# Local attention in a two-block kernel: the second round of transposes starts in another PSUM bank, and one operand split moves one step later

## The chip, the cores and the metric

The kernel runs on one core of a Trainium2 chip. The metric is the time of one execution on the device in microseconds (us). Lower is better. TensorE is called PE in the profile, VectorE DVE, ScalarE ACT, GpSimd POOL and SyncE SP.

## The reference, cut to what matters

The whole program computes two transformer blocks on 512 tokens of width 1024. The first has two kinds of attention and a mixture of experts. The second has a short convolution beside a local (windowed) attention, and then a large product-key feed-forward network. The change lies in the mixer of the second block:

```python
WINDOW = 128
BLOCK = 128
N_HEADS = 8
N_KV_HEADS = 2

def short_conv(b_gate, c_gate, h, conv_w):
    u = c_gate * h
    ...
    y = conv_w[0] * up[:, 0:s]
    for j in range(1, CONV_K):
        y = y + conv_w[j] * up[:, j:j + s]
    return b_gate * y

def window_attention(q, k, v, rel_bias, sinks):
    nb = s // BLOCK
    ...
    kw = with_prev(kb)
    vw = with_prev(vb)
    scores = jnp.einsum('bnqkgd,bnjkd->bnkgqj', qb, kw).astype(jnp.float32) * (HEAD_DIM ** -0.5)
    ...
    m = jnp.maximum(scores.max(axis=-1), sink)
    p = jnp.exp(scores - m[..., None])
    denom = p.sum(axis=-1) + jnp.exp(sink - m)
    o = jnp.einsum('bnkgqj,bnjkd->bnkgqd', p, vw.astype(jnp.float32)) / denom[..., None]

y_conv = short_conv(b_gate, c_gate, hc, conv_w[l])
y_attn = window_attention(q, k, v, rel_bias, sinks[l])
mixed = concatenate([group_rms_norm(y_conv, ...), group_rms_norm(y_attn, ...)])
x = x + g1[:, None] * (mixed @ w_out[l])
```

There are four query blocks of 128 tokens, numbered n = 0 to 3. Each looks at its own 128 keys and, except block 0, at the 128 before them.

## The kernel before

The order of the work is written out by hand: for each stage there is one function per engine (`mix_pe`, `mix_ac`, `mix_dv`), each engine runs its own list in order, and semaphores join them. `F.pe`, `F.ac` and `F.dv` are the counters of the mixer stage. `F.ac["pt", n, kc, 0]` names the point at which ACT has done its copy for block n, key half kc, group 0. `wait_ge` on it holds the engine until that point.

The heart of the mixer is a loop over i = 0 to 11 that all three engines run in step. In step i PE computes the projection chunk 6 + i (`project`, L2232, 24 matmuls of 128x512). Each chunk needs its weights split in two rounded parts by ACT (L2189) and DVE (L2203); `ahead(9 + i)` makes one such pair per step. Between the projections stand the pieces of attention, by the tables `SCORE`, `TURNED`, `VALUES`, `MEANS` and `SCALES`:

- `score(n)`: PE computes the scores of block n (L2275, eight heads in PSUM banks 0 to 3, two heads in each bank). DVE adds the bias and writes them to S8 (L2528), then takes the maximum. ACT takes the exponentials (`exponentials`, L2414).
- `turned(n)`: PE transposes the probabilities (L2291, four 128x128 transposes to a group). For a block with two key halves there are four groups: kc = 0 and kc = 1, each with g = 0 and g = 1. Groups with g = 0 go to bank 6 and are copied out by ACT (L2424), groups with g = 1 go to bank 7 and are copied out by DVE (L2544).
- `values(n)`: PE multiplies with the values into bank 6 (L2301), ACT copies and squares the result (L2436, L2437).
- `means(r)` (L2310, L2313, then L2556, L2557 on DVE, a square root L2441 on ACT and a reciprocal L2559 on DVE), `scales(r)` (L2068 on PE) and `normed(r)` (L2563, L2567 on DVE) are the group norms. ACT's `normed` and DVE's `split` (L2446, L2574) round the result for the output product.
- In the steps 2, 5, 8 and 11 DVE also makes a convolution channel block, `yc` (L2599, L2602, L2606).
- `conv_split(0)` rounds the first half of the normalised convolution for the output product: a copy on ACT (L2455) and a subtraction on DVE (L2580).

After the loop PE runs `begin(0)` and `begin(1)`, the first output products (L2232 again, 6 matmuls each), which read what `conv_split(0)` made, then `scales(2)`, `values(3)`, `begin(2)`, `means(3)`, `begin(3)` and `scales(3)`. The rest of the output product is L2383.

Blocks 1, 2 and 3 are turned in the steps i = 6, 9 and 11. The text calls these place 1, place 2 and place 3.

Of the kernel before, what the change touches and what calls it, by code (L numbers as in the profile page):

```python
# [12 lines left out]
ACT = mybir.ActivationFunctionType  # L13
# [165 lines left out]
def build(nc, A, ctx):  # L179
    with nc.sbuf_tensor("arena", [128, ARENA], F32) as AR:  # L180
        pass
    PS = ctx.enter_context(nc.psum_tensor("psum", [128, 8, 512], F32))
# [41 lines left out]
    IDENT = CST[:, C_ID:C_ID + 128]  # L224
# [1795 lines left out]
    FN, F = Stage(counter, "final", "pe ac dv"), Stage(counter, "mix", "pe ac dv")  # L2020
# [21 lines left out]
    S8 = at3(o, 8, 256)  # L2042
# [171 lines left out]
    def width(n):  # L2214

        return (0, 256) if n else (1, 128)

    def mix_pe(pe):
        final_pe(pe)
        before = [None] * 8  # L2220

        def claim(b):
            if before[b] is not None:
                pe.wait_ge(*before[b])
# [35 lines left out]
        def score(n):  # L2260
            kc0, nk = width(n)
            if n:
                pe.wait_ge(*F.dv["score", n - 1])
                if n == 2:
                    pe.wait_ge(*F.dv["normed", 0])
                if n == 3:
                    pe.wait_ge(*F.dv["normed", 1])
            else:
                pe.wait_ge(*F.dv["q mean"])
                pe.wait_ge(*F.dv["v"])  # L2270
                pe.wait_ge(*F.dv["keys"])
                pe.wait_ge(*F.dv["first", 7])
            for h in range(8):
                j, g = h % 4, h // 4
                pe.matmul(PS[:, h // 2, 256 * (h % 2) + 128 * kc0:256 * (h % 2) + 256],  # L2275
                          Q2[64 * g:64 * g + 64, j, 128 * n:128 * n + 128],
                          K2[64 * g:64 * g + 64, 128 * n + 128 - nk:128 * n + 128], True, True).then_inc(*F.pe("score", n, h))
                if h in (3, 7):
                    pe.wait_ge(*F.pe["score", n, h])

        def turned(n):
            kc0, _ = width(n)
            for kc in range(kc0, 2):
                for g in range(2):
                    if kc == kc0:
                        pe.wait_ge(*F.ac["exp", n])
                        claim(6 + g)
                    else:
                        pe.wait_ge(*(F.dv if g else F.ac)["pt", n, 0, g])
                    for j in range(4):  # L2290
                        ins = pe.transpose(PS[:, 6 + g, 128 * j:128 * j + 128], S8[:, 4 * g + j, 128 * kc:128 * kc + 128], IDENT)  # L2291
                    ins.then_inc(*F.pe("pt", n, kc, g))
            before[6], before[7] = F.ac["pt", n, 1, 0], F.dv["pt", n, 1, 1]

        def values(n):
            kc0, _ = width(n)
# [94 lines left out]
    def mix_ac(ac):  # L2391
        ahead = splits_ac(ac)
        final_ac(ac, ahead)
        ahead(4)
        ac.wait_ge(*F.pe["chunk", 0])
        ac.activation(K2, PS[:, 0, :], ACT.Copy).then_inc(*F.ac("k"))
        ac.activation(KSQ, PS[:, 0, :], ACT.Square).then_inc(*F.ac("k square"))
        ac.wait_ge(*F.pe["chunk", 1])
        ac.activation(VST, PS[:, 1, :], ACT.Copy).then_inc(*F.ac("v"))
        for j in range(4):  # L2400
            ahead(5 + j)
            if j == 2:
                ac.wait_ge(*F.dv["k mean"])
                ac.activation(W1[:, 32:40], W1[:, 32:40], ACT.Sqrt, scale=64.0).then_inc(*F.ac("k root"))
            ac.wait_ge(*F.pe["chunk", 2 + j])
            ac.activation(Q2[:, j, :], PS[:, 4 + j, :], ACT.Copy).then_inc(*F.ac("q", j))
            ac.activation(SQ4[j], PS[:, 4 + j, :], ACT.Square).then_inc(*F.ac("q square", j))

        def exponentials(n):
            kc0, _ = width(n)  # L2410
            ac.wait_ge(*F.dv["max", n])
            ac.activation(ST[:, 16:24], ST[:, 8:16], ACT.Exp)
            for h in range(8):
                ins = ac.activation(S8[:, h, 128 * kc0:256], S8[:, h, 128 * kc0:256], ACT.Exp, bias=ST[:, h:h + 1],  # L2414
                                    accum_out=ST[:, 24 + h:25 + h])
            ins.then_inc(*F.ac("exp", n))

        def turned(n):
            kc0, _ = width(n)
            for kc in range(kc0, 2):  # L2420
                if n:
                    ac.wait_ge(*F.pe["y", n - 1])
                ac.wait_ge(*F.pe["pt", n, kc, 0])
                ac.activation(PT2[kc][0], PS[:, 6, :], ACT.Copy).then_inc(*F.ac("pt", n, kc, 0))  # L2424

        def conv_square(j):
            ac.wait_ge(*F.dv["yc", j])
            if j:
                ac.wait_ge(*F.pe["sums", j - 1])
            ac.activation(CSQ, YC[:, j, :], ACT.Square).then_inc(*F.ac("conv square", j))  # L2430

        def values(n):
            ac.wait_ge(*F.pe["y", n])
            if n:
                ac.wait_ge(*F.pe["sums", n - 1])
            ac.activation(YT2[:, :, 128 * n:128 * n + 128], PS[:, 6, :].rearrange("p (a b) -> p a b", a=4), ACT.Copy)  # L2436
            ac.activation(YSQ, PS[:, 6, :], ACT.Square).then_inc(*F.ac("y square", n))  # L2437

        def roots(r):
            ac.wait_ge(*F.dv["mean", r])  # L2440
            ac.activation(RW, RW, ACT.Sqrt).then_inc(*F.ac("root", r))  # L2441

        def normed(r):
            ac.wait_ge(*F.dv["normed", r])
            for y in range(2):
                ac.activation(parts(YZ[y], 2)[:, 0, :, 128 * r:128 * r + 128], YT2[:, 2 * y:2 * y + 2, 128 * r:128 * r + 128],  # L2446
                              ACT.Copy).then_inc(*F.ac("y split", r, y))

        def conv_split(i):
            if i:  # L2450
                ac.wait_ge(*F.pe["chunk", 17])
            else:
                ac.wait_ge(*F.pe["score", 3, 7])
            ac.wait_ge(*F.dv["conv", 2 * i + 1])
            ac.activation(parts(HCR[i], 2)[:, 0], YC[:, 2 * i:2 * i + 2, :], ACT.Copy).then_inc(*F.ac("conv split", i))  # L2455

        for i in range(12):
            ahead(9 + i)
            if i == 0:
                ac.wait_ge(*F.dv["q mean"])  # L2460
                ac.activation(W1[:, 0:32], W1[:, 0:32], ACT.Sqrt, scale=64.0).then_inc(*F.ac("q root"))
            if i % 3 == 0:
                ac.wait_ge(*F.pe["chunk", 6 + i])
                if i == 0:
                    ac.wait_ge(*F.dv["hn", 7])
                ac.activation(UC[:, i // 3, 2:514], PS[:, 4 + i % 2, :], ACT.Copy).then_inc(*F.ac("uc", i // 3))
            if i == 2:
                exponentials(0)
            if i in (6, 9):
                normed(i // 3 - 2)  # L2470
            if i in TURNED:
                turned(TURNED[i])
            if i in (3, 6, 9):
                conv_square(i // 3 - 1)
            if i in VALUES:
                values(VALUES[i])
            if i in (5, 8, 10):
                exponentials({5: 1, 8: 2, 10: 3}[i])
            if i in MEANS:
                roots(MEANS[i])  # L2480
            if i == 10:
                conv_split(0)
        ahead(22)
        conv_square(3)
        normed(2)
        values(3)
        roots(3)
        normed(3)
        conv_split(1)
        for i in range(8):  # L2490
            ahead(22 + i)
            norm3_squares(ac, i)
        wait_all(ac, F)

    def mix_dv(dv):
# [42 lines left out]
        def turned(n):  # L2538
            kc0, _ = width(n)
            for kc in range(kc0, 2):  # L2540
                if n:
                    dv.wait_ge(*F.pe["y", n - 1])
                dv.wait_ge(*F.pe["pt", n, kc, 1])
                dv.tensor_copy(PT2[kc][1], PS[:, 7, :]).then_inc(*F.dv("pt", n, kc, 1))  # L2544

            dv.wait_ge(*F.ac["exp", n])
            dv.tensor_tensor(ST[:, 24:32], ST[:, 24:32], ST[:, 16:24], ALU.add).then_inc(*F.dv())
            own()
            dv.scalar_tensor_tensor(ST[:, 32:40].rearrange("p (j g) -> p g j", j=4), ST[:, 24:32].rearrange("p (g j) -> p g j", g=2),
                                    EPS, ST[:, 24:32].rearrange("p (g j) -> p g j", g=2), ALU.mult, ALU.mult).then_inc(  # L2550
                *F.dv("eps", n))
# [32 lines left out]
        for i in range(12):  # L2584
# [29 lines left out]
                score(SCORE[i])  # L2614
            if i in MEANS:
                means(MEANS[i])
            if i == 10:
                conv_split(0)
        ahead(22)
        normed(2)  # L2620
# [1253 lines left out]
```

## Time and profile before

| | |
|---|---|
| time of three runs | 2625.12, 2632.83, 2634.41 us; median 2632.83 |
| profiled execution, its own time | 2622.8 us |
| its span, first to last instruction | 2621.1 us |
| around the span | 1.7 us |
| PE busy | 2374.4 us, 91% of the span |
| DVE busy | 1615.3 us, 62% |
| ACT busy | 866.5 us, 33% |
| mean granted TensorE clock | 0.962 of full |

The busy time is a sum over stages with different limits, so it does not tell what a single edit is worth. The chain of waits does: it goes back from the last instruction, at each step to what released it. The mixer's loop runs from about 1178 to 1294 us of the span.

### The profile page before, as it was taken

To read this page: it belongs to the slowest core of one execution; us is meant where nothing else is said; L and a number is where in the kernel's file an instruction comes from. 1 tells how busy PE (TensorE), PEld (TensorE's weight loads), DVE (VectorE), ACT (ScalarE), POOL (GpSimd) and SP (SyncE) were. 2 spreads that over 40 slices of the span, in tenths; PEclk is the share of its full clock that TensorE was granted. 3 is DMA by queue.
4 is the path that set the end of the run, shared out by engine and by line. 5 is a ranking of instruction groups with operands and counts; after the bars stand their busy time and mean duration, and the time that the engine had idled before them with its cause. 6 is when DMAs were issued, how large, how long until landed. Compare 5 with 4: busy or idle time off the path is not lost.

```text
span 2621.1 us, 32694 instructions
## 1 busy us (share of the span) xinstructions
PE 2374.4 (91%) x12845; PEld 1785.9 (68%) x12845; DVE 1615.3 (62%) x3288; ACT 866.5 (33%) x1619; POOL 859.2 (33%) x700
## 2 busy tenths in 40 slices
PE   8998888997987777699899967799999999999999
PEld 7755555675544444377675656688888888888887
DVE  5357576443101000155527999699889888899986
ACT  3134343531000000133421248643434333333332
POOL 0013321001110010000001169475567766666760
PEclk9999899998999999889999978899999999999999
DMA  4345010347999999731122006899999999999993
GB/s 189 125 171 193 33 65 33 131 161 302 426 426 426 427 427 426 291 123 65 65 110 108 25 21 246 299 413 345 359 396 413 414 412 413 381 405 398 397 402 125
DMA packets 137551, 693.68 MB, mean 265 GB/s; under 512 B 18364, under 2 KB 36836, under 8 KB 103600
## 3 DMA queue, kind: packets, MB, share of 16 engines
q1 hardware_dynamic: 76656, 479.68, 46.0%
q0 software_dynamic: 60736, 211.85, 20.7%
q8 instruction: 103, 1.69, 0.3%
q14 instruction: 56, 0.46, 0.1%
HBM read 659.52 MB, written 38.81 MB: 266 GB/s over the span
## 4 chain that ended last, share of the span: by engine, by line
PE 64%; DVE 17%; DMA 15%; ACT 3%; issue 1%; SPq 0%; POOL 0%; DVEq 0%; POOLq 0%; ACTq 0%
PE psum L3453 13%; DMA arena<-w 13%; PE psum L3418 11%; PE psum L2770 4%; PE psum L2232 4%; PE psum L466 4%; PE psum L982 3%; PE psum L1703 3%; DVE arena L3668 2%; PE psum L3424 2%; PE psum L3422 2%; DVE arena L877 2%; DVE rounded L3551 2%; PE psum L1283 2%; PE psum L1298 2%; PE psum L2383 2%
## 5 line engine op out<-in xcount | busy, mean ns | idle before, releaser
L3453 PEld LDWEIGHTS psum<-rounded,rounded 128*128 128x128 f32 x2880 | 432.1, 189 | 23.6 <-ACT rounded L3500 10.9
L3453 PE MATMUL psum<-rounded,rounded 128*128 128x320 f32 x2880 | 445.1, 311 | 1.0 <-ACT arena L3529 0.7
L3418 PE MATMUL psum<-rounded,rounded 128*128 128x512 f32 x1536 | 398.7, 396 | 2.8 <-DVE rounded L3571 2.5
L3364 POOL DMA_INDIRECT arena<-u_rows,arena x192 | 288.4, 1502 | 174.0 <-DVE arena L3668 53.4
L3418 PEld LDWEIGHTS psum<-rounded,rounded 128*128 128x128 f32 x1536 | 283.5, 189 | 80.1 <-issue 14.3
L3364 POOL DMA_INDIRECT arena<-v_rows,arena x192 | 288.0, 1500 | 151.0 <-DVE arena L3679 68.7
L3551 DVE TENSOR_TENSOR rounded<-arena,rounded 128x1024 fp32r<-128x1024 f32 x248 | 302.8, 1221 | 5.7 <-ACT rounded L3486 5.7
L1703 PE MATMUL psum<-arena 128*64 128x256 f32 x2048 | 234.5, 384 | 60.6 <-DMA arena<-w 59.8
L1831 DVE COPY arena<-psum 128x256 f32<-128x256 f32 x32 | 13.6, 425 | 407.3 <-PE psum L1770 407.3
L3486 ACT ACTIVATE rounded<-arena 128x1024 fp32r<-128x1024 f32 x248 | 260.0, 1049 | 11.0 <-DMA arena<-uv 10.9
L1703 PEld LDWEIGHTS psum<-arena 128*64 128x64 f32 x2048 | 148.7, 138 | 157.5 <-DMA arena<-w 62.8
L3499 ACT ACTIVATE rounded<-arena 128x320 fp32r<-128x320 f32 x128 | 60.5, 473 | 336.6 <-PE psum L3418 241.8
L1678 POOL DMA_INDIRECT yb<-arena x32 | 31.8, 994 | 415.0 <-ACT arena L1817 401.2
L3679 DVE SCALAR_TENSOR_TENSOR arena<-arena 128x1024 f32<-128x1024 f32 x127 | 162.6, 1281 | 3.8
L3673 DVE CUSTOM_DVE_ANT_0 arena<-arena 128x1024 f32<-128x1024 f32 x128 | 153.3, 1221 | 0.0
L1714 PE MATMUL psum<-arena 128*64 128x512 f32 x512 | 116.9, 598 | 26.4 <-DVE arena L1836 12.0
L2998 PE MATMUL psum<-arena 128*128 128x128 f32 x640 | 96.1, 308 | 34.9 <-DVE arena L3152 20.0
L3529 ACT ACTIVATE arena<-psum 128x320 f32<-128x320 f32 x120 | 52.2, 435 | 208.4 <-PE psum L3453 208.4
L1817 ACT ACTIVATE arena<-psum 128x512 f32<-128x512 f32 x32 | 19.1, 597 | 298.8 <-PE psum L1714 298.8
L2232 PE MATMUL psum<-rounded 128*128 128x512 f32 x456 | 115.5, 411 | 1.9 <-DVE rounded L2128 1.8
L2998 PEld LDWEIGHTS psum<-arena 128*128 128x128 f32 x640 | 86.7, 216 | 44.2 <-DVE arena L3152 24.2
L2770 PE MATMUL psum<-arena 128*128 128x512 f32 x256 | 115.3, 605 | 1.7 <-ACT arena L2809 1.7
(498 smaller groups left out, 3764.3 us busy)
## 6 DMA issues: line engine op xcount, KB each, us to landing
arena<-w SPq DMA_DIRECT2D x96, 2048.0 KB, 42.1
arena<-uv SPq DMA_DIRECT2D x124, 1024.0 KB, 8.4
arena<-wada SPq DMA_DIRECT2D x12, 2048.0 KB, 9.7
arena<-gd SPq DMA_DIRECT2D x30, 640.0 KB, 7.0
arena<-wp SPq DMA_DIRECT2D x8, 2048.0 KB, 7.7
gd<-arena SPq DMA_DIRECT2D x11, 1024.0 KB, 10.8
arena<-win SPq DMA_DIRECT2D x4, 2048.0 KB, 8.2
arena<-wq SPq DMA_DIRECT2D x4, 2048.0 KB, 9.4
```

What stands on the lines that cost most here:

```text
L1703: ins = pe.matmul(PS[64 * half:64 * half + CAP, b, 0:256], xt[:, k, x0:x0 + CAP], wt[:, k, 256 * half:256 * half + 256], k == 0, k == 7)
L1714: ins = pe.matmul(PS[64 * half:64 * half + CAP, b, :], ht[:, kt % 2, 64 * (kt // 2):64 * (kt // 2) + CAP], w2[:, kt, 512 * half:512 * half ...
L2232: ins = pe.matmul(PS[:, b, :], w[:, x, k, :], h[:, y, k % 2, :], k == 0 and m == 0, k == 7 and m == 2)
L2770: ins = pe.matmul(PS[:, f, :], w[:, k, 128 * f:128 * f + 128], H2[:, k, :], k == 0, k == 7)
L2998: ins = pe.matmul(PS[:, b, 128 * x:128 * x + 128], BH[i][:, x, :], AH[i][:, x, :], True, True)
L3364: po.indirect_dma_start(out=ROWS_OF[i % len(ROWS_OF)], out_offset=None, in_=src, in_offset=bass.IndirectOffsetOnAxis(ap=column.bitcast(U32 ...
L3418: ins = pe.matmul(PS[:, 2 * n + half, :], gg[:, z, 128 * n:128 * n + 128], v[:, y, 512 * half:512 * half + 512], x == 0 and i == 0, x == 1 ...
L3453: ins = pe.matmul(PS[:, 7, 0:DT], w[:, y, k, :], hv[:, z, :], k == 0 and i == 0, k == 7 and i == 2)
L3486: ac.activation(SPL[j % 5][:, 0:1024], at(RAW[(j // 2) % 3] + 1024 * (j % 2), 1024), ACT.Copy).then_inc(*E.ac("split", j))
L3551: dv.tensor_tensor(s[:, 1024:2048], at(RAW[(j // 2) % 3] + 1024 * (j % 2), 1024), s[:, 0:1024].bitcast(F32), ALU.subtract).then_inc(*E.dv( ...
L3673: dv.tensor_tensor_reduce(row, row, H2T, 1.0, 0.0, ALU.mult, ALU.add, ZS[:, k:k + 1]).then_inc(*E.dv("dot", k))
L3679: dv.scalar_tensor_tensor(H2T, row, ZS[:, k:k + 1], H2T, ALU.mult, ALU.add).then_inc(*E.dv("sum", k))
```

## The change

There are two edits. First, a new function `turn_bank` picks the bank of each group of transposes. The first round of a block stays in banks 6 and 7. In the second round (kc = 1, blocks 1 to 3) group 0 goes to bank 3, which held two heads of the scores, so it no longer waits for ACT's copy of the first round; group 1 stays in bank 7. `score(n)` now waits for ACT's copy of bank 3 from block n - 1. Second, `conv_split(0)` moves from step 10 to step 11 on both ACT and DVE, behind the copies of the last transposes and the means.

```diff
+    def turn_bank(kc, kc0, g):
+
+        return 6 + g if g or kc == kc0 else 3
+
...
             if n:
                 pe.wait_ge(*F.dv["score", n - 1])
+                pe.wait_ge(*F.ac["pt", n - 1, 1, 0])
...
                 for g in range(2):
+                    b = turn_bank(kc, kc0, g)
                     if kc == kc0:
                         pe.wait_ge(*F.ac["exp", n])
-                        claim(6 + g)
-                    else:
-                        pe.wait_ge(*(F.dv if g else F.ac)["pt", n, 0, g])
+                        claim(b)
+                    elif g:
+                        pe.wait_ge(*F.dv["pt", n, 0, 1])
                     for j in range(4):
-                        ins = pe.transpose(PS[:, 6 + g, 128 * j:128 * j + 128], S8[:, 4 * g + j, 128 * kc:128 * kc + 128], IDENT)
+                        ins = pe.transpose(PS[:, b, 128 * j:128 * j + 128], S8[:, 4 * g + j, 128 * kc:128 * kc + 128], IDENT)
                     ins.then_inc(*F.pe("pt", n, kc, g))
-            before[6], before[7] = F.ac["pt", n, 1, 0], F.dv["pt", n, 1, 1]
+            before[6], before[7] = F.ac["pt", n, kc0, 0], F.dv["pt", n, 1, 1]
...
-                ac.activation(PT2[kc][0], PS[:, 6, :], ACT.Copy).then_inc(*F.ac("pt", n, kc, 0))
+                ac.activation(PT2[kc][0], PS[:, turn_bank(kc, kc0, 0), :], ACT.Copy).then_inc(*F.ac("pt", n, kc, 0))
...
-            if i == 10:
+            if i == 11:
                 conv_split(0)
...
-                dv.tensor_copy(PT2[kc][1], PS[:, 7, :]).then_inc(*F.dv("pt", n, kc, 1))
+                dv.tensor_copy(PT2[kc][1], PS[:, turn_bank(kc, kc0, 1), :]).then_inc(*F.dv("pt", n, kc, 1))
...
-            if i == 10:
+            if i == 11:
                 conv_split(0)
```

The lines below the new function are 4 to 6 numbers higher in the changed kernel: L2291 becomes L2297, L2275 becomes L2280, L2232 becomes L2236, L2544 becomes L2550, L2580 becomes L2586, L2455 becomes L2461 and L2424 becomes L2430.

The first piece is PE's list at place 2: the scales, the transposes of block 2 and the scores of block 3, first before, then changed.

```order
1372 L2068 MATMUL psum<-arena 64x128 [waits mix_dve]
1374 L2291 MATMUL psum<-arena 128x128 [waits mix_act]
1375 L2291 MATMUL psum<-arena 128x128 x7
1376 L2291 MATMUL psum<-arena 128x128 [waits mix_act]
1377 L2291 MATMUL psum<-arena 128x128 x3
1378 L2291 MATMUL psum<-arena 128x128 [waits mix_dve]
1379 L2291 MATMUL psum<-arena 128x128 x3
1380 L2275 MATMUL psum<-arena 128x256 x4
```

```order
1372 L2068 MATMUL psum<-arena 64x128 [waits mix_dve]
1374 L2297 MATMUL psum<-arena 128x128 [waits mix_act]
1375 L2297 MATMUL psum<-arena 128x128 x11
1376 L2297 MATMUL psum<-arena 128x128 [waits mix_dve]
1377 L2297 MATMUL psum<-arena 128x128 x3
1378 L2280 MATMUL psum<-arena 128x256 [waits mix_act]
1379 L2280 MATMUL psum<-arena 128x256 x3
```

Twelve transposes stand behind the first wait in place of eight, the wait on ACT between the rounds is gone, the wait on DVE stays, and the scores have a wait on ACT of their own. Places 1 and 3 read alike but for what follows them.

The second piece is DVE's list from step 10 to the end of the loop, before and changed. The name rounded_2048 with 128x1024 stands both for a weight split (L2203) and for the convolution's split (L2580, then L2586).

```order
847 L2595 TENSOR_TENSOR arena<-arena,psum 128x512 [waits mix_pe]
848 L2580 TENSOR_TENSOR rounded_2048<-arena,rounded_2048 128x1024 [waits mix_act]
849 L2203 TENSOR_TENSOR rounded_2048<-arena,rounded_2048 128x1024 [waits mix_act]
850 L2599 TENSOR_SCALAR arena<-arena 128x512 [waits mix_dve]
852 L2606 TENSOR_TENSOR arena<-arena,psum 128x512 [waits mix_dve,mix_pe]
853 L2544 COPY arena<-psum 128x512 [waits mix_pe] x2
856 L2556 TENSOR_SCALAR arena<-psum 128x8 [waits mix_dve,mix_pe]
857 L2557 TENSOR_TENSOR arena<-psum,arena 128x8
858 L2559 RECIPROCAL arena<-arena 128x16 [waits mix_act]
859 L2203 TENSOR_TENSOR rounded_2048<-arena,rounded_2048 128x1024 [waits mix_act] x2
```

```order
847 L2601 TENSOR_TENSOR arena<-arena,psum 128x512 [waits mix_pe]
848 L2203 TENSOR_TENSOR rounded_2048<-arena,rounded_2048 128x1024 [waits mix_act]
849 L2605 TENSOR_SCALAR arena<-arena 128x512 [waits mix_dve]
851 L2612 TENSOR_TENSOR arena<-arena,psum 128x512 [waits mix_dve,mix_pe]
852 L2550 COPY arena<-psum 128x512 [waits mix_pe] x2
855 L2562 TENSOR_SCALAR arena<-psum 128x8 [waits mix_dve,mix_pe]
856 L2563 TENSOR_TENSOR arena<-psum,arena 128x8
857 L2565 RECIPROCAL arena<-arena 128x16 [waits mix_act]
858 L2586 TENSOR_TENSOR rounded_2048<-arena,rounded_2048 128x1024 [waits mix_act]
859 L2203 TENSOR_TENSOR rounded_2048<-arena,rounded_2048 128x1024 [waits mix_act] x2
```

The convolution's split moved from ahead of the step's weight split to behind the reciprocal of the means. The same move stands in ACT's list, where the copy L2461 now follows the square root.

The third piece is PE's list behind the last transposes: the two sums of `means(2)`, `begin(0)` with `begin(1)`, and `scales(2)`, before and changed.

```order
1394 L2310 MATMUL psum<-arena 128x2 x4
1395 L2313 MATMUL psum<-arena 128x2 x4
1396 L2232 MATMUL psum<-rounded_2048 128x512 x12
1397 L2068 MATMUL psum<-arena 64x128 [waits mix_dve]
1398 L2068 MATMUL psum<-arena 64x128 x15
```

```order
1391 L2316 MATMUL psum<-arena 128x2 x4
1392 L2319 MATMUL psum<-arena 128x2 x4
1393 L2236 MATMUL psum<-rounded_2048 128x512 [waits mix_dve]
1394 L2236 MATMUL psum<-rounded_2048 128x512 x11
1395 L2068 MATMUL psum<-arena 64x128 x16
```

The wait on DVE stands now ahead of the first output product and no longer ahead of the scales.

## Rows read from the trace of the kernel before

**Rows 1.** The page, part 4: shares of the chain by engine and by line

```profile
PE 64%; DVE 17%; DMA 15%; ACT 3%; issue 1%; SPq 0%; POOL 0%; DVEq 0%; POOLq 0%; ACTq 0%
PE psum L3453 13%; DMA arena<-w 13%; PE psum L3418 11%; PE psum L2770 4%; PE psum L2232 4%; PE psum L466 4%; PE psum L982 3%; PE psum L1703 3%; DVE arena L3668 2%; PE psum L3424 2%; PE psum L3422 2%; DVE arena L877 2%; DVE rounded L3551 2%; PE psum L1283 2%; PE psum L1298 2%; PE psum L2383 2%
```

**Rows 2.** Chain of waits at place 1: start us, us, what

```profile
1229.70 1.04 DVE arena L2567 x4
1230.75 0.02 issue
1230.77 0.72 ACT rounded L2446 x2
1231.49 0.49 ACT arena L2424
...
1232.03 1.36 PE psum L2291 x8
1233.39 6.78 PE psum L2232 x24
```

**Rows 3.** Timeline of DVE at place 1: start us, us, what

```profile
1230.65 0.68 DVE L2544 COPY arena<-psum 128x512 f32<-128x512 f32 x1
```

**Rows 4.** Timeline of PE, places 1 and 2: in brackets the idle time before

```profile
1228.84 1.09 PE L2291 MATMUL psum<-arena 128*128 128x128 f32 x8
1232.03 1.36 PE L2291 MATMUL psum<-arena 128*128 128x128 f32 x8 [2.10 <-ACT arena L2424]
...
1246.07 5.73 PE L2232 MATMUL psum<-rounded 128*128 128x512 f32 x24
...
1264.11 1.09 PE L2291 MATMUL psum<-arena 128*128 128x128 f32 x8 [2.10 <-ACT arena L2424]
```

**Rows 5.** Windows: length, busy us per engine, granted clock, DMA

```profile
1230.00:1232.00 2.00, 0.00 (x0) 0.00 (x0) 1.33 (x4) 1.21 (x3) 0.00 (x0) 1.00 0.00 0
...
1234.00:1236.00 2.00, 2.00 (x6) 1.57 (x5) 1.97 (x6) 0.78 (x1) 0.00 (x0) 0.50 0.00 0
...
1264.00:1266.00 2.00, 1.89 (x12) 1.64 (x13) 0.76 (x2) 1.25 (x4) 0.00 (x0) 1.00 0.10 41
...
1290.00:1292.00 2.00, 1.67 (x9) 1.67 (x9) 0.79 (x2) 0.00 (x0) 0.00 (x0) 0.50 0.00 0
```

**Rows 6.** Chain of waits at place 2

```profile
1263.58 0.49 ACT arena L2424
...
1265.20 1.94 PE psum L2275 x8
```

**Rows 7.** Chain of waits from `values(2)` through place 3

```profile
1276.90 0.60 ACT arena L2436
1277.50 0.49 ACT arena L2437
...
1284.42 1.22 DVE rounded L2580
1285.65 1.15 DVE rounded L2203
...
1290.33 1.12 PE psum L2291 x4
1291.45 1.50 PE psum L2310 x8
1292.95 1.71 PE psum L2313 x8
1294.65 4.29 PE psum L2232 x12
```

**Rows 8.** Timeline of ACT and of DVE behind the square root of `means(2)`

```profile
1295.09 1.99 ACT L2189 ACTIVATE rounded<-arena 128x1024 fp32r<-128x1024 f32 x2
...
1296.16 2.36 DVE L2203 TENSOR_TENSOR rounded<-arena,rounded 128x1024 fp32r<-128x1024 f32 x2 [0.69 <-ACT rounded L2189]
```

**Rows 9.** L2232 in 1234:1236: duration ns min/median/max, first and last start

```profile
L2232 PE MATMUL psum<-rounded x6: 571/628/629, 1233.6 to 1235.7; 128*128 128x512 f32 x6
```

## The prediction

> **What bounds the kernel now.** I read the page's chain shares first [rows 1]. PE holds 64% of the chain that ended last, and the mixer's projections (L2232) are 4% of the span. So the mixer is a part in which PE sets the pace, and an edit counts only where PE stands still. I then took the chain of waits through the mixer's loop, piece by piece. It is PE from 1179 to 1290 us but for three stretches, and these are exactly the three places of `turned`. At place 1 the chain leaves PE for the norm on DVE (L2567), the rounding on ACT (L2446) and ACT's copy of bank 6 (L2424), and comes back to PE at 1232.03 [rows 2]; PE had been idle 2.10 us [rows 4]. Place 2 is the same picture with the same 2.10 us [rows 4], with the chain again over ACT's copy [rows 6]. At place 3 the chain runs through ACT's exponentials, then the convolution's split and the weight split on DVE, and back to PE at 1290.33 [rows 7]. Last I looked at the granted clock. At place 1 it is full while PE stands idle and half of full (1.2 instead of 2.4 GHz) soon after the restart; at place 2 it stays full after an equally long idle; at place 3 it is half [rows 5].
>
> **The change, part by part.**
>
> Place 1, the wait. The four transposes of the second round's group 0 no longer wait for ACT, so they run straight behind the first eight, in time in which PE was idle. Group 1 still waits for DVE's copy of bank 7, which starts at 1230.65 and takes 0.68 [rows 3], so it is done at 1231.33. PE restarts about 0.05 later, as it does now behind ACT (1231.98 to 1232.03 [rows 2]), at 1231.38. Four transposes take half of 1.09 [rows 4], so the projection behind them starts at about 1231.92. Now it starts at 1233.39 [rows 2]. That is -1.47.
>
> Place 1, the clock. The projection after the restart took 6.78 us [rows 2], where the same 24 matmuls take 5.73 at full clock [rows 4], a loss of 1.05. I call it -1.1 with rounding of the overlapping ends. With an idle of about 0.9 us instead of 2.10 I expect the clock to stay up. That is a choice: the lower bound is nothing, since the clock fell after one gap of 2.10 us and not after the other. With it, place 1 gives -2.6.
>
> The Trainium skill bears on this choice. Its page "TensorE: Matmul & The Clock Gate", Part 1, says that the throttle follows recent PE activity, but that the count of slow matmuls is "run-variable", because the hardware's observation is not aligned to the kernel. The pair of equal gaps with unequal clocks in rows 5 agrees. By the page alone place 1 would be -1.5 in an average execution and the total near zero.
>
> Place 2. The scores of block 3 follow the transposes at once, and now wait for ACT's copy of bank 3. ACT's first copy starts at 1263.58 by the chain and ends at 1264.07; the second follows it at the pitch of back-to-back copies, 0.49 [rows 6, 7], so it ends at 1264.56 and PE starts the scores near 1264.6. Now they start at 1265.20 [rows 6]. That is -0.6. Here the new wait eats more than half of what the old one cost. At places 1 and 3 nothing is lost to it: a projection of 5.73 us [rows 4] lies between ACT's copy and the next scores, or there are no next scores. If that cover were gone, place 1 would lose the same 0.5.
>
> Place 3, the gain. DVE does the convolution's split first, from 1284.42, then the weight split at 1285.65 less an overlap of about 0.1, and then the convolution block and the copy that PE waits for [rows 7]. Without the split ahead of it that whole row moves up by one DVE instruction pitch, 1.15. On ACT the split's copy went first too, so the weight copy is ready as early as the split's copy was; DVE does not wait longer. The freed group 0 transposes bring nothing more, because DVE is last in any case. PE comes back at 1289.18 in place of 1290.33 [rows 7]: -1.15.
>
> Place 3, the new wait. The split is now behind the reciprocal of `means(2)` on DVE, and its copy behind the square root on ACT. But `begin(0)`, next on PE behind the sums, reads it. Before, the sums' end and `begin(0)` are both 1294.65 [rows 7]. ACT is free for its next 128x1024 copy at 1295.09, and DVE starts its subtraction on such a copy at 1296.16 [rows 8]. The split's subtraction takes 1.22 [rows 7]. So it is done at 1297.38, and PE starts `begin(0)` at 1297.42 by the old clock of events: +2.77. Behind that waiting matmul are `begin(1)`, `scales(2)`, `values(3)` and the rest of the output product, all delayed by it; DVE's `normed(2)` waits for `scales(2)`, and ACT's rounding for that. The two weight splits behind (ACT 1.99, DVE 2.36 us [rows 8]) run under `begin(0)` and `begin(1)` (4.29 us) and stay hidden. The weights of `begin(0)` and `begin(1)` are split before.
>
> Place 3, the clock. PE restarts at half clock either way, after some 4 us of idle. The sums and transposes (1.12, 1.50, 1.71) are slow now [rows 7] and I leave them so. The 12 matmuls of the first products take 4.29. All at half clock they would take 12 x 0.42 = 5.0 (the pitch is 2.1 us over 5 [rows 9]), all at full 12 x 5.73 / 24 = 2.9. The extra stand of 2.8 us can only put off the recovery, so I take half of the way up, +0.4. If the new phase brings the full clock early, it is up to -1.4 there and some -2.1 on the sums and transposes (they take 4.33; at half of it each they would take 2.2).
>
> Sum: -2.6 - 0.6 - 1.15 + 2.77 + 0.4 = -1.2 us. No DMA is moved. Behind the mixer the chain goes on over PE and DVE to the feed-forward network, so the shift reaches the end unchanged. Against the profiled execution, 2622.8, that makes 2621.6; against the median of the three runs it makes 2631.6. The four executions known have their middle at 2629.0 ((2625.12 + 2632.83) / 2), less 1.2 is 2627.8. Between the two I say 2630.
>
> **The rivals.** *Net slower*: the new wait of `begin(0)` wins. It costs 2.77 and with an all-slow first product 3.5. If the clock at place 1 falls in spite of the shorter idle (-1.5 instead of -2.6), the sum is -1.5 - 0.6 - 1.15 + 2.77 + 0.75 = +0.3; if also DVE's copy at place 1 starts only when ACT's rounding ends (0.72 us [rows 2]), it is +1.0, so about 2633 to 2634. It decides once the wait with its slow clock costs more than the 4.35 won before. For it: the split and its two hops ACT to DVE to PE stand in full on the path with nothing ahead to hide them. Against: places 1 and 2 are clean arithmetic.
>
> *Clock luck to the other side*: at place 3 the clock rises before the first product. Then -1.2 - 0.4 - 1.4 - 2.1 = -5, about 2626. For it: the level after a gap is not tied to the gap's length alone [rows 5]. Against: at place 3 the idle stays at 4 us.
>
> *Absorbed*: what is won early is lost to a later fixed point, for instance a weight that DMA brings no sooner (DMA is 15% of the chain [rows 1]). Then the time is the old one, 2632.8. Against: in the mixer the chain has no DMA.
>
> *The change does nothing at places 1 and 2*, since DVE's copy ends nearly with ACT's: the difference of their ends is only 0.65 us (1231.33 against 1231.98). Then only place 3 counts, -1.15 + 3.17 = +2.0, about 2635. Against: the four transposes taken into the idle time are worth 0.5 by themselves.
>
> **How the numbers follow.** Forecast 0.45 (between -2.5 and 0), net slower 0.20, clock luck 0.15, absorbed 0.12, nothing at places 1 and 2 0.08. All of them are between -5 and +2 us. A measurement of this kernel tells about 0.5% from no change, 13 us, so no case reaches a verdict by itself; what is left is the spread of executions, 2622.8 to 2634.4. Same 0.93, faster 0.04, slower 0.03. The range takes the spread and the ends of the cases: 2625.1 - 5 = 2620 at the low end, 2634.4 + 2 and some width for a spread known from four executions, 2640, at the high end.
>
> **What would show it.** Place 1: PE's idle before the last four transposes (L2297) about 0.9 us, released by DVE L2550 and no longer by ACT, and the clock at 1.00 in the following projection. Place 2: the scores L2280 released by ACT L2430, with 0.5 us or so idle before. Place 3: one idle of about 4 us released by DVE L2550, then a new idle of 2.8 us ahead of the first L2236 of the output product, released by DVE L2586. From the start of `scales(0)` at place 1 to the first L2389 the stretch should be 1.2 us shorter. The prediction is wrong if `begin(0)` does not wait, if place 1 gives under 1 us, or if the time moves by more than 13 us.

## The result and the profile after

The changed kernel took 2631.85 us (median of 20 runs), the kernel before 2626.52 us in the 20 runs beside it. The ratio is 1.0017 with a 95% interval of 1.0009 to 1.0024: slower by 4.5 us (0.17% of 2626.5; the two medians differ by 5.3), where I had forecast 1.2 us less. Two repeats (below) gave 0.9997 and 1.0000. The time is inside my range, the sign is not the one forecast. Four executions in this record took over 3000 us; they are left out of every ratio.

The chain of waits of the changed kernel at place 1, at place 3 and behind it (start us, us, what):

```profile
1237.58 0.61 DVE arena L2550
...
1238.23 0.66 PE psum L2297 x4
1238.89 5.48 PE psum L2236 x24
...
1292.22 0.61 DVE arena L2550
1292.83 0.04 issue
1292.88 1.11 PE psum L2297 x4
1293.99 1.50 PE psum L2316 x8
1295.49 1.72 PE psum L2319 x8
...
1297.72 0.95 ACT rounded L2461
1298.67 0.03 issue
1298.70 1.24 DVE rounded L2586
1299.93 0.04 issue
1299.98 5.49 PE psum L2236 x12
```

Beside [rows 2] and [rows 7] nearly every wait is where the prediction put it. PE's timeline shows the idle times themselves:

```profile
1238.23 0.66 PE L2297 MATMUL psum<-arena 128*128 128x128 f32 x4 [1.02 <-DVE arena L2550]
...
1268.82 4.04 PE L2280 MATMUL psum<-arena 64*128 64x256 f32 x16 [0.47 <-ACT arena L2430]
...
1292.88 1.11 PE L2297 MATMUL psum<-arena 128*128 128x128 f32 x4 [4.16 <-DVE arena L2550]
...
1299.98 5.49 PE L2236 MATMUL psum<-rounded 128*128 128x512 f32 x12 [2.78 <-DVE rounded L2586]
```

The new wait ahead of the first output product is 2.78 us (forecast 2.77 to 2.8), the scores wait 0.47 for ACT, and place 1's stand is down from 2.10 to 1.02.

I call S the stretch from the first L2068 of place 1 to the first matmul of the rest of the output product. It is 85.5 us in the profile of before and 85.2 in this one: 0.3 us less. Yet the span of this profile is 8.5 us longer (2629.6 against 2621.1). Of that, 6.8 lie ahead of S (it starts at 1233.8, before at 1226.9), where both programs run the same instructions, and 2.0 behind it. So one pair of profiles can't explain the result, and the profile of before, with 2622.8 us, was at the low end of the times of its kernel (2622.17 to 2634.41 in 20 runs).

### The profile page after: what moved, and what is told of

It is laid out like the page before. It is cut to its first block, busy times and chain, and to the rows that moved or that the text cites. A ratio compares the mean times of both kernels' runs of the same rounds, so it can differ in the third digit from the quotient of the medians.

```text
span 2629.6 us, 32693 instructions
## 1 busy us (share of the span) xinstructions
PE 2385.4 (91%) x12845; PEld 1792.3 (68%) x12845; DVE 1615.0 (61%) x3288; ACT 866.9 (33%) x1619; POOL 857.2 (33%) x700
## 4 chain that ended last, share of the span: by engine, by line
PE 65%; DVE 16%; DMA 15%; ACT 3%; issue 1%; SPq 0%; POOL 0%; DVEq 0%; POOLq 0%; ACTq 0%
PE psum L3459 13%; DMA arena<-w 13%; PE psum L3424 11%; PE psum L2776 4%; PE psum L466 4%; PE psum L2236 4%; PE psum L982 3%; PE psum L1703 3%; DVE arena L3674 2%; PE psum L3430 2%; PE psum L3428 2%; DVE rounded L3557 2%; PE psum L1283 2%; PE psum L1298 2%; PE psum L2389 2%; DVE arena L3155 1%
## 5 line engine op out<-in xcount | busy, mean ns | idle before, releaser
L2236 PE MATMUL psum<-rounded 128*128 128x512 f32 x456 | 115.1, 408 | 5.7 <-DVE rounded L2128 2.8
```

The source lines that it names most:

```text
L2236: ins = pe.matmul(PS[:, b, :], w[:, x, k, :], h[:, y, k % 2, :], k == 0 and m == 0, k == 7 and m == 2)
```

## The experiments

Each timed kernel has 7 to 12 runs beside 23 to 35 of the kernel before on the same chip. S was read from each kernel's profile in the same way.

**The two edits apart, and a null.** `e1_banks` is the changed kernel with the split back in step 10, and with a wait of its own for bank 3:

```diff
-            if i == 11:
+            if i == 10:
                 conv_split(0)
...
-        before[3] = F.dv["score", 3]
+        before[3] = F.ac["pt", 3, 1, 0]
```

> The bank edit alone: the convolution's split is back in step 10; begin(0) also waits for ACT's last copy of bank 3, long done by then. S is the stretch from the first L2068 of place 1 to the first L2383 (L2389): 85.4 us before, 85.1 us in the changed kernel. Theory A (the loss is the new wait of the first output product at place 3 and the slow clock behind it): S near 82.2 (85.4 - 2.6 - 0.6, 1.5 either way by the clock), time 1 to 4 us under before. Theory B (the loss lies outside the stretch, in how the program's instructions lie or in the phase of the clock): S the same 82.2, but the time 2 to 5 us above before, as the changed kernel's.

`e2_split` is the kernel before with `if i == 11: conv_split(0)` on ACT and DVE.

> The move of the convolution's split alone, banks as before. Theory A: S near 87.0 to 88.5 (85.4 - 1.15 + 2.77, and up to 1.5 of slow clock), time 2 to 5 us above before. Theory B: S the same, but the time no further above before than the changed kernel's, and in the trace the stretches ahead of the mixer longer than before's.

`e3_between` is the changed kernel with the split moved within step 11:

```diff
             if i in TURNED:
                 turned(TURNED[i])
+            if i == 11:
+                conv_split(0)
...
             if i in MEANS:
...
-            if i == 11:
-                conv_split(0)
```

> Both edits, but the split stands in step 11 between the copies of the last transposes and the means, where DVE had 2.2 us idle. Theory A: no wait ahead of begin(0), S near 81.1 (85.4 - 2.6 - 0.6 - 1.15), time 3 to 6 us under before. Theory B: S 81.1 but the time about that of the changed kernel or 1 us below it, above before.

`e4_null` adds two waits to the kernel before, `pe.wait_ge` on `F.ac["hn", 0]` and `FN.dv["both"]`, behind `final_pe`.

> The kernel before with two waits on PE at the start of the mixer that are met at once or shortly; no other instruction moves. It shifts the PE instruction stream of all that follows. Theory A: S 85.4, time that of before within 2 us. Theory B in its form of code placement: 3 us or more away from before, with S 85.4.

| kernel | ratio to before | interval | S, us |
|---|---|---|---|
| e1_banks | 0.9992 | 0.9981 to 1.0004 | 86.1 |
| e2_split | 1.0003 | 0.9992 to 1.0014 | 86.4 |
| e3_between | 0.9991 | 0.9981 to 1.0001 | 85.5 |
| e4_null | 1.0001 | 0.9988 to 1.0013 | 85.3 |

None differs from before in time, and the null excludes nothing but a large effect of where the instructions lie. The traces say more. In e1 and e3 S is 3.9 and 4.4 us over what I expected, and 3.2 us of that are in one place: the scores of block 3 and the projection behind them ran slow. The rest is in the first output products, which took 5.02 and 5.47 us where the profile of before has 4.43. In e2 and e4, with the old order at place 2, the scores and their projection did not run slow. S of e2, 86.4, is below the 87.0 to 88.5 that I expected, because I had counted from the profile of before, in which the clock fell at place 1; in e2 it did not.

**The changed kernel again (e5, e10), and fillers (e6 to e8).** Fillers are extra matmuls put where PE stands idle, here matmuls of 512 columns into a free bank, whose results nobody reads:

```diff
+        def fill(w, bank, count):
+            pe.wait_ge(*F.dv["w", w])
+            for _ in range(count):
+                pe.matmul(PS[:, bank, :], parts(WSPF[w % 4], 8)[:, 0, 0, :], parts(HNR[3], 2)[:, 0, 0, :], True, True)
...
+                        fill({1: 13, 2: 16, 3: 18}[n], 0, 16 if n == 3 else 4)
...
+        fill(18, 1, 10)
         begin(0)
...
         scales(3)
+        fill(21, 6, 12)
```

That is e7. In e6 (the kernel before) eight stand in the 2.10 us at places 1 and 2, and 4 and 14 at place 3; there, as in e8 (e3 with fillers), none stands ahead of `begin(0)`. The twelve behind `scales(3)` are in all three.

> The changed kernel again, unaltered, on a chip of this call. Theory A (the edits themselves cost more than they bring, as the first comparison's 1.0017 says): a ratio of 1.001 to 1.0025 to the kernel before. Theory C (the first comparison lay at an end of what the clock's phase makes of an execution; the two edits apart add to -1.3 us): a ratio of 0.999 to 1.0005. S (first L2068 of place 1 to first L2389) between 84 and 89 in either.

> The kernel before with filler matmuls of 512 columns, whose results nobody reads, in PE's idle times at the three places and ahead of the first L2383. They add work that the reference does not have and take none away. Theory C (the clock at half rate is a large and chance part of S): the granted clock is 1.00 through the stretch, S 81.5 to 82.5 with the sums (1.50 and 1.71 before) at 0.8 and 0.9 and the first products at 2.9 us, L2383's first 54 matmuls at 12.8; time 3 to 5 us under before. Theory A: S falls by under 2 us.

> The changed kernel with the same kind of filler matmuls, also in the new wait ahead of the first output product. With the clock out of the comparison, S less S of the kernel before with fillers is the waits alone: -1.2 - 0.6 - 1.15 + 2.77 = -0.2 (place 1's gain is 1.2 and not 1.47 where the old transposes run at full clock). Theory A: +2 or more. Time within 1.5 us of the filled kernel before.

> Both edits, with the split between the last copies and the means, and fillers in the idle times. Its wait ahead of begin(0) is gone: S 2.8 us under the changed kernel with fillers (near 79.0), the time 2 to 4 us under it and 5 to 8 us under the kernel before. If the wait ahead of begin(0) is not what it seems, S is less than 1.5 us under.

| kernel | ratio to before | interval | S, us |
|---|---|---|---|
| e5_again (changed) | 0.9997 | 0.9988 to 1.0006 | 88.6 |
| e10_again2 (changed) | 1.0000 | 0.9987 to 1.0013 | 88.7 |
| e6_before_fill | 0.9976 | 0.9964 to 0.9988 | 82.1 |
| e7_after_fill | 0.9990 | 0.9980 to 1.0001 | 84.9 |
| e8_between_fill | 0.9976 | 0.9965 to 0.9988 | 83.2 |

The fillers did not keep the clock up everywhere, as I had expected. In e7 and e8 it fell at place 2 as in e5, though four fillers stood in the 1.03 us ahead of the last transposes there: scores and projection took 3.2 us more than in e6. That is why S of e7 is 2.8 us over e6 and not 0.2 under. S of e8 is 1.7 us under e7 and not 2.8: its wait ahead of `begin(0)` is down to 0.51 us, but the first output products took 4.62 us, in e7, behind ten fillers, 3.30.

The chain of e10, the changed kernel, at place 2:

```profile
1262.57 0.98 ACT arena L2430 x2
1263.55 0.04 issue
1263.60 2.00 PE psum L2280 x8
1265.60 0.04 issue
1265.65 3.00 PE psum L2280 x8
1268.65 0.04 issue
1268.69 7.91 PE psum L2236 x24
```

and its windows there (length, busy us per engine, granted clock, DMA share, GB/s):

```profile
1263.00:1265.00 2.00, 1.53 (x9) 1.23 (x8) 1.80 (x6) 2.00 (x4) 0.00 (x0) 1.00 0.08 33
1265.00:1267.00 2.00, 1.94 (x8) 1.37 (x7) 1.53 (x5) 0.01 (x1) 0.00 (x0) 0.87 0.00 0
1267.00:1269.00 2.00, 1.94 (x5) 1.04 (x5) 1.17 (x3) 0.00 (x0) 0.00 (x0) 0.50 0.00 0
```

The clock falls to half in the second half of the scores; these take 3.00 in place of 2.00 and the projection 7.91 in place of 5.73, together 3.2 us. Ahead of the fall PE had stood 1.03 and 0.47 us around four transposes. The same fall is in e5. The first profile of the changed kernel is the exception: its clock is 1.00 in each window from 1270 to 1276, and its scores took 4.04 us.

**The order at place 2 undone (e9), fillers ahead of the scores (e11), and the best guess (e12).**

```diff
-        return 6 + g if g or kc == kc0 else 3
+        return 6 + g if g or kc == kc0 or n == 2 else 3
```

e9 is the changed kernel with this (the function takes n too) and the old waits at place 2; e12 is e3 with the same. e11 is e7 with `fill(16, 0, 4)` ahead of the wait of `score(3)`.

> The changed kernel, but at place 2 alone the second round's group 0 is back in bank 6 and the scores' new wait is gone. In five of six profiles with the new order at place 2 the clock fell in or just behind the scores of block 3, in none of four with the old order. Theory D (that fall, 3.3 us, is the part of the loss that the sum lacked): scores of block 3 in 4.0 us and the projection behind them in 5.7, S 85.5 to 86.5 (the repeat of the changed kernel had 88.5), time 1 to 4 us under the changed kernel of this call. Theory A (place 3 alone is the loss): S and time 0.6 us above the changed kernel's.

> The changed kernel a third time, unaltered. Theory D: the clock falls at place 2 in most executions, S 88 to 89 where it does and 85 to 86 where it doesn't, a ratio of 1.0005 to 1.0015 to the kernel before. Theory C (the first comparison was chance): 0.9990 to 1.0003.

> The changed kernel with fillers (as in the earlier run) and four more matmuls ahead of the scores of block 3, where PE stood 0.47 us. They cost about 0.6 us by themselves. Theory D: the clock stays at 1.00 there, S near 82.2 where the filled kernel without them had 84.9. Theory A: S 85.4, the four matmuls' own time more.

> The new bank at places 1 and 3, the old order at place 2, the convolution's split between the last copies and the means. Theory D: S 85.3 - 1.2 - 1.15 = 83.0, time 2 to 4 us under the kernel before, the best without fillers. Theory A: S the same but for the 0.6 us that place 2 gives up, time no better than the version with both edits and the split between, 1.3 us under before.

Theory D says that the new order at place 2 makes the clock fall and the old one does not. e11 came out as theory D said: S 82.1, the clock at 1.00. It was run once, so its time (2619.0 us) has no ratio.

```profile
1261.83 0.66 PE psum L2305 x4
1262.49 0.92 PE psum L2291 x4
1263.41 1.94 PE psum L2282 x8
...
1265.39 2.00 PE psum L2282 x8
...
1267.44 5.74 PE psum L2236 x24
```

Four useless matmuls ahead of the scores (L2291 here) took 2.8 us off S against e7. They also put the scores 0.4 us later, so e11 alone can't tell whether PE's work or the shift kept the clock up; e15 below answers that in part. But the other two sank theory D. e9 was 1.0019 (1.0003 to 1.0034) and e12 1.0020 (1.0009 to 1.0030), slower than the changed kernel beside them. e12's S is 89.1 us and not 83.0. In its trace the clock fell at place 2 with the old order: transposes, scores and projection took 1.96, 7.51 and 7.66 us. The profile of e9 has S 85.4, no fall there, and the time 2626.8; nine of its other eleven runs are slower than that, seven of them at 2635 to 2639. So the old order is no cure; in e12 the clock fell there too, and at a higher price (some 6 us and not 3.2).

**A wait less, and extra work (e13 to e15), and the version that follows (e16).** Theory E says that the clock changes at nearly fixed points of the program's time, and that a stand of PE costs clock or not by where it lies against them. e13 is the kernel before with the new bank in place 1 only (`or n > 1 else 3`, the split in step 10). e14 is e9, and e15 the changed kernel, with `if i == 6: fill(13, 0, 5)` or `fill(13, 0, 2)` behind `turned`. e16 is e8 with e11's four matmuls.

> The kernel before with the new bank at place 1 alone: 1.2 us of wait less there, all else as before. Theory E (the mixer starts at nearly the same point of the clock's own decisions in most executions, and what a wait at place 2 costs in clock depends on where it lies against them; a shift of 1.2 us moves the 2.10 us stand of place 2 onto one): the clock falls at place 2 in most executions, S 90 to 92, time 2 to 6 us above before though a wait was taken away. Theory D (the new order at place 2 makes the clock fall, the old never): S 84.1, time 1.2 us under before.

> The version with the old order at place 2 (1.0019 to before, with most of its times at 2635 to 2639), and five matmuls of 512 columns that nobody reads behind the transposes of place 1, 1.2 us of pure extra work, so that place 2 lies where it lay in the kernel before. Theory E: S 86 to 87 in the profile, the times fall by 3 us or more to 2627 to 2632, in spite of the extra work. Theory D or plain noise: 1.2 us slower, or no change.

> The changed kernel with two such matmuls behind the transposes of place 1: 0.5 us of extra work, place 2 0.5 us later. In the changed kernel's own profile the clock did not fall at place 2, and it alone had its clock changes 0.3 us earlier against the mixer. Theory E: no fall at place 2 in the profile, S 85.4 to 86.0 and times 1 to 3 us under the changed kernel's 2629. Theory D: the fall stays, S 89.1.

> Both edits, the split between the last copies and the means, and fillers in every stand of PE, those ahead of the scores of block 3 too. No clock fall in the stretch but the one behind the means: S 79.5 to 80.5, against 82.1 of the filled kernel before; time 7 to 10 us under the kernel before, the best of all. Theory D and E agree here; if the waits' arithmetic is off, S is over 81.5.

| kernel | ratio to before | interval | S, us |
|---|---|---|---|
| e13_place1_only | 1.0016 | 1.0006 to 1.0027 | 89.6 |
| e14_p2old_nudge | 1.0022 | 1.0009 to 1.0035 | 86.4 |
| e15_after_nudge | 1.0018 | 1.0007 to 1.0029 | 85.6 |
| e16_both_filled | 0.9970 | 0.9959 to 0.9980 | 81.6 |

e13 shortens a wait at place 1, leaves the order at place 2 as it was, and is slower, by 0.16%, about what repeats of one kernel differ by; its trace is the firmer evidence. Its chain and windows at place 2:

```profile
1269.13 1.97 PE psum L2300 x8
1271.10 3.72 PE psum L2281 x8
...
1274.87 3.79 PE psum L2281 x8
...
1278.70 7.55 PE psum L2236 x24
```

```profile
1268.00:1270.00 2.00, 0.87 (x4) 0.87 (x5) 0.43 (x1) 1.08 (x3) 0.00 (x0) 0.73 0.63 270
1270.00:1272.00 2.00, 2.00 (x8) 1.53 (x7) 0.83 (x3) 1.72 (x3) 0.00 (x0) 0.50 0.00 0
```

At place 1 it won its 1.1 us. At place 2 the 2.10 us stand is the same as before, but the clock falls in it, and transposes, scores and projection take 1.97 + 7.51 + 7.55 in place of 1.09 + 4.04 + 5.73, some 6 us more. The one thing that changed at place 2 is when it comes.

e15 is the counterpart. Against e5 only two matmuls at place 1 are added, which put the scores of place 2 0.5 us later; the stands of 1.03 and 0.46 us are still there, and the clock does not fall:

```profile
1264.50 4.04 PE L2280 MATMUL psum<-arena 64*128 64x256 f32 x16 [0.46 <-ACT arena L2437]
```

So a later place 2 is enough to keep the clock up, without fillers in the stands. S of e16, 81.6, is above the 79.5 to 80.5 that I expected: PE still waited 0.32 us ahead of `begin(0)`, and the first output products ran at half clock, in 5.49 us.

**The kernel before against itself (e17), and e14 again (e18).**

> The kernel before, unaltered, timed against itself: what the comparison gives for no change, and a second profile of it. Theory E: S 85.0 to 85.6 with no clock fall at places 1 and 2. A ratio outside 0.9990 to 1.0010 would mean that the small differences seen so far are partly the comparison's own.

> The version with the old order at place 2 and five useless matmuls behind place 1, again. Theory E: S 86 to 87 with no fall at place 2, and a ratio of 1.0000 to 1.0010 (S 1 us over before). If the ratio is again near 1.002 with S 86.4, something outside the stretch makes these versions slower and theory E covers the stretch alone.

e17: ratio 0.9992 (0.9980 to 1.0005), S 85.2, no fall at places 1 and 2. e18: 1.0011 (1.0001 to 1.0020), S 85.8, no fall. So theory E was right on the clock at place 2 in e13, e14, e15, e17 and e18 (S of e13 and e18 is 0.4 and 0.2 us under what I had given for it). Its times held in e13; in e14 and e15 they did not come down. e18 is the same kernel as e14, and its 1.0011 lies in the interval of e14.

These ratios are small beside what repeats show: the changed kernel gave 1.0017, 0.9997 and 1.0000 in three comparisons. A single ratio of 1.0016 to 1.0022 (e9, e12 to e15) is therefore weak evidence, and the argument rests on the traces.

**What the twenty profiles say together.** I measured everything against the first L2068 of place 1. The last fall of the clock ahead of it lies 47.2 to 47.9 us earlier in 18 of 20 profiles. It is 45.4 in the profile of before (1181.5 to 1226.9) and 48.1 in e9's. The windows of before and of e10 show it, 0.63 against 0.54 in the same two microseconds, though the loop of e10 comes 1.6 us later:

```profile
1181.00:1183.00 2.00, 2.00 (x11) 1.81 (x11) 0.55 (x2) 0.67 (x3) 0.00 (x0) 0.63 0.00 0
```

```profile
1181.00:1183.00 2.00, 2.00 (x10) 1.90 (x10) 0.31 (x2) 0.38 (x2) 0.00 (x0) 0.54 0.00 0
```

So the clock's changes are nearly fixed to the program's own time here, though not wholly. Then the start of the scores of block 3 tells whether it fell there:

| start of the scores, us behind the first L2068 | order at place 2 | profiles | clock fell there |
|---|---|---|---|
| 36.6 to 36.7 | old | e2, e4, e6, e14, e17, e18 | none |
| 38.2 | old, after a fall at place 1 | before | none |
| 35.6, or 36.5 behind slow transposes | old | e9, e12, e13 | e12, e13 |
| 35.0 | new | after, e1, e3, e5, e7, e8, e10 | all but after |
| 35.4 to 35.5 | new, with extra matmuls | e11, e15, e16 | none |

Two profiles stand apart from those with the same place 2: after from the six that fell, and e9 from e12 and e13. In both the last fall ahead of the mixer lies further off, 47.9 and 48.1 us, where it is 47.2 to 47.6 in the eight that fell. That fits theory E: they have the same stands, but 0.3 to 0.9 us elsewhere against the clock's changes.

## Why the prediction was wrong, point by point

The terms are read from two profiles, both by the chain of waits: of the kernel before one without a fall at place 1 (e17), of the changed kernel one with the fall at place 2 (e5). e17:

```profile
1231.31 1.92 PE psum L2068 x32
...
1237.42 5.49 PE psum L2232 x24
...
1267.95 1.94 PE psum L2275 x8
...
1277.71 1.91 PE psum L2301 x8
...
1293.07 1.11 PE psum L2291 x4
...
1297.39 5.33 PE psum L2232 x12
...
1316.45 14.38 PE psum L2383 x54
```

and e5:

```profile
1236.80 1.92 PE psum L2068 x32
...
1241.85 5.48 PE psum L2236 x24
...
1271.76 2.00 PE psum L2280 x8
...
1284.73 1.91 PE psum L2307 x8
...
1298.96 1.11 PE psum L2297 x4
...
1306.07 5.49 PE psum L2236 x12
...
1325.28 14.37 PE psum L2389 x54
```

**Place 1, the wait, was right.** From the first L2068 to the projection it is 6.11 us in e17 (1231.31 to 1237.42) and 5.05 in e5 (1236.80 to 1241.85), -1.06. I had -1.47, of which 0.3 were slow transposes in the profile of before that e17 does not have.

**Place 1, the clock: this step failed first.** I took the fall of the clock in the profile of before as the usual case and counted -1.1 for its end, nearly the whole of my -1.2. In the profiles of e2, e4 and e17, with the old order and no fillers, the clock does not fall at place 1. There was nothing to win in them.

**Place 2: -0.6 was right for the wait, and the term for the clock was missing. This is the step that turned the sum.** From the projection of place 1 to the scores it is 30.53 us in e17 and 29.91 in e5, -0.62. But scores and projection then take 12.97 in e5 against 9.76 in e17 (1267.95 to 1277.71), +3.21. I had asked of the clock only at the stands that the change shortens, and taken a shorter stand to be safe. The fall came behind two short stands, at a place that had been moved.

**Place 3.** The gain was -1.15 and is -1.13 (15.36 us from `values(2)` to the restart in e17, 14.23 in e5). The new wait was +2.77 and is +2.79 (sums and wait 7.11 against 4.32). The clock term was +0.4 against a first product of 4.29 us; in e17 that product takes 5.33, in the changed kernel 5.49, so the change adds only +0.15 with all that follows. Against the profile of before, from which I had forecast, this term was too small: from the first product to L2389 the first profile of the changed kernel takes 18.96 us (1299.98 to 1318.94), before 17.77 (1294.65 to 1312.42), which is +1.2 and not +0.4. With -2.6 at place 1, -0.6, about -1.1 and +2.8 as forecast, that makes the 0.3 us less of the first pair. That place 1 gave its -2.6 there was luck: the fall that the change seems to end is one that e2, e4 and e17 do not have.

The sum with these: -1.06 - 0.62 + 3.21 - 1.13 + 2.79 + 0.15 = +3.34 us, which is S of e5 less S of e17 (88.48 - 85.14 by these lines). Without the fall at place 2 it is about 0: 3.34 - 3.21 = +0.13. The three comparisons of the changed kernel, 4.5, -0.8 and 0 us, average 1.8 us weighted by their 20, 12 and 12 runs. Two falls in three unfilled profiles would give 3.34 - 3.21 / 3 = 2.3. These agree, but three profiles are no proof of a share, and the first comparison's own 4.5 us are not explained: its profile has no fall at place 2.

**Rivals.** *The change does nothing at places 1 and 2* is refuted by -1.06 and -0.62. *Absorbed* does not fit either: from the first L2389 (L2383) to the end e5 takes 1309.9 us, e10 1310.3 and e17 1310.4, so nothing behind the mixer made up for a longer S. The new wait of `begin(0)` stands on the path in full, as the rival had it, but costs 1.7 us net of its own gain and does not decide alone. My reason for "clock luck" was that the clock's level after a gap is not tied to the gap's length. That held, with the other sign and at place 2, and its 3.2 us are the largest term of the difference between e5 and e17. The rule of the Trainium skill that I weighed ("TensorE: Matmul & The Clock Gate", Part 1) says that the count of slow matmuls varies between runs. That agrees with the spread of S of the changed kernel, 85.2 to 88.7, but by variation between runs alone no start of place 2 would be favoured. The table says otherwise: with the scores at 35.0 us the clock fell in six of seven profiles, with the scores at 36.6 to 36.7 in none of six.

**What stays open.** Why e14 and e15, whose profiles show S within 1.2 us of before, were timed at 1.0022 and 1.0018. One profile per kernel can't tell whether most of their executions had another pattern. The times don't tell either: the first L2068 of place 1 starts at 1226.9 to 1236.7 us in the twenty profiles, so what happens ahead of the mixer moves an execution by up to 9.8 us. The execution of e5 that I took apart was the slowest of its twelve (2636.97, median 2626.79), that of e10 a middle one (2629.25, median 2629.16), and both have the fall. The kernel before against itself gave 0.9992, and the changed kernel's three comparisons spread over 0.2%, so their 0.2% may be the comparison's own. That the fall depends on where place 2 lies is shown by the traces of e13 and e15 beside those with the same stands in the table, one execution of each. Whether PE's work ahead of the scores decides too is not shown: e11 and e16 filled the stand and moved the scores at once. What fixes the clock's changes to the program ahead of the mixer was not tried.

## What to carry to other kernels

Before a clock loss in a profile goes into a sum, find out whether the usual execution has it: a null edit or a second profile of the same kernel costs one run. A microsecond won upstream can cost six downstream, by moving a stand of PE to where the clock falls (e13), so an edit of that size must be judged by the stretch behind it too. Filling the stands with matmuls that nobody reads was worth more than taking the stands away. The fillers alone (e6) ran at 0.9976 of before (0.9964 to 0.9988), with S 82.1; both edits with the split moved (e3) at 0.9991 (0.9981 to 1.0001), with S 85.5. e16 with both ran at 0.9970 (0.9959 to 0.9980); that it beats e6 is not shown, since the intervals overlap. Of the 6.3 us of e6 3.1 are in S against e17, and 1.6 behind it, where the first 54 matmuls of L2383 took 12.83 us and not 14.38.

## What was not expected of the hardware

The clock fell after two stands of 1.03 and 0.47 us with four transposes between them (e5, e10), even with fillers in the first of them (e7, e8), and not after either of the two stands of 2.10 us in e17. At place 3 the granted clock stayed at half through 4.3 us in which PE was busy without a gap, with transposes and matmuls of two columns. In the profile of before it rose in the output product behind them (0.50 at 1294 to 1296, 1.00 at 1298 to 1300); in e17 it stayed at half through that whole product (5.33 us) and was at 0.95 only at 1303 to 1305. And the last fall ahead of the mixer kept its distance to the first L2068 of place 1 to within 0.8 us in 18 of 20 executions, on several chips, while that L2068 itself moved between 1226.9 and 1236.7 us of the span.
